# Recurrent rows turned inside the mixer's loop, first gate pieces placed around the last attention units, and a shorter wait ahead of the output projection

## What is computed

```python
y_m = mlstm_chunkwise(q_m, k_m, v_m, log_i, log_f)      # 4 recurrent heads, 256 wide each
y_m = sigmoid(o_m) * y_m
y_a = chunk_causal_mla_attention(q_nope, q_rope, k_nope, k_rope, v_a)   # 8 heads, 128 wide each
g_m, g_a = split(sigmoid(gate_pre), 2)
merged = g_m * (y_m @ w_branch_m) + g_a * (y_a @ w_branch_a)
x = x + gate1 * (merged @ w_out)
```

## Time and profile before

| what | value |
|---|---|
| median of 3 runs (lowest, highest) | 1639.94 us (1638.41, 1641.69) |
| span of the profiled execution | 1638.2 us |
| PE busy | 1520.7 us, 93% of the span |
| DVE, ACT, POOL busy | 47%, 28%, 35% |
| share of PE in the chain that ended last | 84% |
| recurrent loop, first to last unit, with the latent thirds | 871.4 to 938.2 us |
| `yT` strips turned and split | 938.2 to 945.2 us |
| `gm`, `bm` | 945.2 to 1033.2 us |
| attention loop | 1087.5 to 1169.8 us |
| last `yaT` strips | 1170.7 to 1173.4 us |
| `ga`, `ba` | 1173.4 to 1262.2 us |
| `wout` begins | 1266.9 us |

### The profile page before, as it was taken

One profiled execution on the slowest core, in us unless ns is written; L12 is line 12 of the kernel. 1 busy time (PEld: TensorE's weight loads), 2 busy tenths in 40 slices (PEclk: granted clock), 3 DMA queues, 4 the chain that ended last, 5 costly groups with the idle time before them and its releaser, 6 DMA issues.

```text
span 1638.2 us, 21248 instructions
## 1 busy us (share of the span) xinstructions
PE 1520.7 (93%) x8362; PEld 1199.8 (73%) x8362; DVE 769.3 (47%) x1470; ACT 455.3 (28%) x722; POOL 579.8 (35%) x473
## 2 busy tenths in 40 slices
PE   6989998999999999989999999999999989887885
PEld 5978887878888888857888878775688866554442
DVE  2475656378686863238215620445313254423234
ACT  4352334242231313143323232342223121000001
POOL 2571220435454444434533144520154323312222
PEclk9998999999999999989999999999999999989997
DMA  4241110325435442313222122210043689999995
GB/s 166 91 185 49 52 52 1 111 109 212 184 155 206 167 167 103 109 52 109 104 97 71 40 78 103 90 53 23 26 166 143 259 332 353 377 397 373 394 412 200
DMA packets 37347, 260.91 MB, mean 159 GB/s; under 512 B 7280, under 2 KB 7920, under 8 KB 13184
## 3 DMA queue, kind: packets, MB, share of 16 engines
q1 hardware_dynamic: 31488, 251.13, 40.7%
q0 software_dynamic: 5760, 8.41, 1.6%
HBM read 252.69 MB, written 17.30 MB: 165 GB/s over the span
## 4 chain that ended last, share of the span: by engine, by line
PE 84%; DVE 7%; issue 4%; ACT 3%; POOL 1%; DMA 1%; DVEq 0%; SPq 0%; ACTq 0%; POOLq 0%
PE G L2090 13%; PE G L2091 13%; PE G L2092 13%; PE G L2624 4%; PE SA L2624 4%; PE SA L2090 3%; PE SA L2092 3%; PE SA L2091 3%; PE PB L2092 3%; PE PB L2091 3%; PE PB L2090 3%; PE OB L2280 2%; PE G L2132 2%; PE SA L2513 1%; PE PB L2632 1%
## 5 line engine op out<-in xcount | busy, mean ns | idle before, releaser
L753 POOL TENSOR_TENSOR wl<-raw,wh 128x512 fp32r<-128x512 f32 x356 | 479.9, 1379 | 674.5 <-ACT wh L885 669.6
L885 ACT ACTIVATE wh<-raw 128x2048 fp32r<-128x2048 f32 x90 | 172.3, 1915 | 298.7 <-PE SA L2092 153.7
L2090 PE MATMUL G<-Hh,wh 128*128 128x512 f32 x544 | 217.7, 400 | 4.6 <-DVE Yl L1837 1.6
L2091 PE MATMUL G<-Hl,wh 128*128 128x512 f32 x544 | 214.4, 394 | 0.0
L2092 PE MATMUL G<-Hh,wl 128*128 128x512 f32 x544 | 214.3, 394 | 0.0
L1593 DVE SCALAR_TENSOR_TENSOR arena<-arena,st 128x256 f32<-128x256 f32 x144 | 132.9, 923 | 5.1
L2090 PEld LDWEIGHTS G<-Hh,wh 128*128 128x128 f32 x544 | 103.8, 191 | 25.7 <-DVE Yl L1837 1.9
L2092 PEld LDWEIGHTS G<-Hh,wl 128*128 128x128 f32 x544 | 103.5, 190 | 22.6
L2091 PEld LDWEIGHTS G<-Hl,wh 128*128 128x128 f32 x544 | 103.6, 190 | 19.9
L825 POOL DMA_INDIRECT raw<-xn_rows,arena x38 | 36.8, 967 | 129.4 <-PE G L2640 104.9
L2090 PE MATMUL G<-wh,Hh 128*128 128x256 f32 x256 | 76.6, 299 | 0.0
(11 more groups left out here) (528 smaller groups left out, 3111.5 us busy)
## 6 DMA issues: line engine op xcount, KB each, us to landing
raw<-in_pieces_dram SPq DMA_DIRECT2D x91, 1024.0 KB, 4.8
arena<-in_pieces_dram SPq DMA_DIRECT2D x24, 1024.0 KB, 4.8
arena<-in_wexp_dram SPq DMA_DIRECT2D x11, 2048.0 KB
dn_w<-in_wexp_dram SPq DMA_DIRECT2D x18, 1024.0 KB, 42.0
arena<-in_wexp_dram SPq DMA_DIRECT2D x12, 1024.0 KB, 30.3
gu_y<-in_wexp_dram SPq DMA_DIRECT2D x6, 2048.0 KB
gu_z<-in_wexp_dram SPq DMA_DIRECT2D x5, 2048.0 KB
gu_h<-in_wexp_dram SPq DMA_DIRECT2D x4, 2048.0 KB
```

What stands on the lines that cost most here:

```text
L753: ins = pool.tensor_tensor(low_[:, part], whole[:, part], high[:, part], ALU.subtract)
L885: act.activation(split_pair(s)[0], wait_raw(act, sp_list[s]), ACT.Copy).then_inc(S("high_split"), 1)
L2090: pe.matmul(out, ah, bh, start=first, stop=False)
L2091: pe.matmul(out, ah, bl, start=False, stop=False)
```

## The change

- **Recurrent rows.** Strips 0 and 1 (head 0) are turned at the end of step 8, strips 2 and 3 (head 1) at the end of step 12, strips 4 and 5 (head 2) in step 17. Strips 6 and 7 (head 3) are turned between the first and the second `gm` group. The latent thirds 16 and 17 stand inside steps 16 and 17, each ahead of an `mvalues`. ACT and DVE split the strips at their steps 9, 13 and 17. The PE loop has 18 steps. `bm`'s first group waits strip by strip.
- **Latent rows.** The sums of squares stand behind the second `gm` group on ACT and write to another scratch tile; POOL makes the roots behind the split of three more pieces instead of one; DVE scales behind the fourth `bm` group.
- **Attention.** The first `ga` group is cut in two halves: k 0 to 3 ahead of the last `avalues`, k 4 to 7 behind it. The strips of block 3 are turned behind it, then comes the second `ga` group.
- **Output projection.** Pieces 0 and 2 wait for four strips of `merged`, pieces 1 and 3 for all eight.

```diff
     g += [("vm", t, "a") for t in range(8)]
-    g += [("c3", t, "a") for t in range(6)]
-    g += [("yT", f, "v") for f in range(KT)]
+    for i in range(6):
+        g += [("c3", i, "a")]
+        if i in (2, 4, 5):
+            g += [("yT", 2 * (i // 2 - 1) + n + (2 if i == 5 else 0), "v") for n in range(2)]
+    g += [("gm", 0, "a"), ("yT", 6, "v"), ("yT", 7, "v"), ("gm", 1, "a")]
...
-    g += [("yaT", i, "v") for i in range(8)]
+    g += [("yaT", i, "v") for i in range(6)]
+    g += [("ga", 0, "a"), ("yaT", 6, "v"), ("yaT", 7, "v"), ("ga", 1, "a")]
...
+        MIXED_AT = {9: (0, 1), 13: (2, 3), 17: (4, 5)}
...
-            low(sp_list[NC3])
+            for p in sp_list[NC3:NC3 + 3]:
+                low(p)
             pool.wait_ge(S("ss_c"), 1)
...
+            def mixed_high(f):
+                b = wait_group(act, "yT", f)
+                act.activation(Yhv[:, f, :], b[:, :], ACT.Copy, scale=0.5).then_inc(S("yT_high"), 1)
...
                 if t < len(munits):
                     munit(t)
+                if t in MIXED_AT:
+                    for f in MIXED_AT[t]:
+                        mixed_high(f)
...
                     free_group(act.activation(tg[:, f, :], b[:, :], ACT.Tanh, scale=0.5), "gm", i)
+                    if i == 0:
+                        mixed_high(6)
+                        mixed_high(7)
                 high(s)
                 s += 1
+                if j == 0:
+                    latent_squares()
...
             for j in range(4):
                 high(s)
                 s += 1
...
                     free_group(act.activation(tga[:, f, :], b[:, :], ACT.Tanh, scale=0.5), "ga", i)
+                    if i == 0:
+                        attended_high(3)
...
+            def mixed_low(f):
+                b = wait_group(dve, "yT", f)
+                dve.wait_ge(S("yT_high"), f + 1)
+                free_group(dve.scalar_tensor_tensor(Ylv[:, f, :], b[:, :], 0.5, Yhv[:, f, :].bitcast(F32), ALU.mult, ALU.subtract), "yT", f)
...
                 if 0 <= t - 1 < len(munits):
                     mcopied(t - 1)
+                if t in MIXED_AT:
+                    for f in MIXED_AT[t]:
+                        mixed_low(f)
+            mixed_low(6)
+            mixed_low(7)
...
-            for t in range(len(munits) + 3):
+            def mixed_turned(h):
+
+                pe.wait_ge(S("m_out"), 4 * h + 4)
+                for f in range(2 * h, 2 * h + 2):
+                    transposes("yT", f, [To[:, t, f * P:(f + 1) * P] for t in range(NT)])
+
+            for t in range(len(munits) + 2):
                 if t < len(munits):
                     mscores(t)
                 if t < 16:
                     c3_third(t)
+                if t == 17:
+                    c3_third(17)
+                    mixed_turned(2)
                 if 0 <= t - 1 < len(munits):
                     mturned(t - 1)
+                if t == 16:
+                    c3_third(16)
                 if 0 <= t - 2 < len(munits):
                     mvalues(t - 2)
-            for t in (16, 17):
-                c3_third(t)
-            pe.wait_ge(S("m_out"), len(munits))
-            for f in range(KT):
-                transposes("yT", f, [To[:, t, f * P:(f + 1) * P] for t in range(NT)])
-            wait_freed(pe, "yT", KT - 1)
+                if t in (8, 12):
+                    mixed_turned(t // 4 - 2)
+            one_feature("gm", ("gm", 0), 0, 0)
+            mixed_turned(3)
+            one_feature("gm", ("gm", 0), 1, 1)
             for j in range(4):
-                features("gm", ("gm", j), 2 * j)
-                features("bm", ("bm", j), 2 * j, act=(Yhv, Ylv))
+                if j:
+                    features("gm", ("gm", j), 2 * j)
+                features("bm", ("bm", j), 2 * j, act=(Yhv, Ylv), source=None if j else "yT")
...
-            for t in range(len(aunits) + 4):
...
+            for t in range(len(aunits) + 2):
...
+                if t == len(aunits) + 1:
+                    one_feature("ga", ("ga", 0), 0, 0, range(4))
                 if 0 <= t - 2 < len(aunits):
                     avalues(t - 2)
+            one_feature("ga", ("ga", 0), 0, 0, range(4, KT))
+            attended_turned(3)
+            one_feature("ga", ("ga", 0), 1, 1)
             wait_freed(pe, "yaT", 7)
...
-            pe.wait_ge(S("merged_low"), KT)
             for j in range(4):
+                pe.wait_ge(S("merged_low"), KT if j % 2 else KT // 2)
                 wide_rows("wout", ("wout", j), 4 * (j // 2), j % 2)
```

More of the change, by code:

```diff
@@ L188, in plan_groups @@
     g += [("va", i, "a") for i in (6, 7)]
-    g += [("yaT", i, "v") for i in range(8)]
+    g += [("yaT", i, "v") for i in range(6)]
+    g += [("ga", 0, "a"), ("yaT", 6, "v"), ("yaT", 7, "v"), ("ga", 1, "a")]
     for j in range(4):
-        g += [("ga", 2 * j + f, "a") for f in range(2)]
+        if j:
+            g += [("ga", 2 * j + f, "a") for f in range(2)]
         g += [("ba", 2 * j + f, "v") for f in range(2)]
@@ L813, in _ @@
             pool.tensor_tensor(rsc, msc, mhalf.to_broadcast([P, 8]), ALU.pow).then_inc(S("rstd_c"), 1)
-            for p in sp_list[NC3 + 1:]:
+            for p in sp_list[NC3 + 3:]:
                 low(p)
@@ L1160, in aunit, with attended_high @@
                                accum_out=rsum2[:, (q % 2) * 8 + h:(q % 2) * 8 + h + 1]).then_inc(S("probs_ready"), 1)
+            def attended_high(q):
+                for i in range(2):
+                    b = wait_group(act, "yaT", 2 * q + i)
+                    act.activation(Yhv[:, 4 * i:4 * i + 4, q * P:(q + 1) * P], b[:, :].rearrange("p (f n) -> p f n", f=4), ACT.Copy).then_inc(S("yaT_high"), 1)
             for t in range(len(aunits) + 4):
@@ L1167, in _ @@
                     aunit(t)
-                if t >= 11 and (t - 11) % 8 == 0:
-                    q = (t - 11) // 8
-                    for i in range(2):
-                        b = wait_group(act, "yaT", 2 * q + i)
-                        act.activation(Yhv[:, 4 * i:4 * i + 4, q * P:(q + 1) * P], b[:, :].rearrange("p (f n) -> p f n", f=4), ACT.Copy).then_inc(S("yaT_high"), 1)
+                if t >= 11 and (t - 11) % 8 == 0 and t < len(aunits):
+                    attended_high((t - 11) // 8)
             for j in range(4):
@@ L1760, in _ @@
                 free_group(dve.scalar_tensor_tensor(merged[:, i, :], tg[:, i % 2, :], 1.0, b[:, :], ALU.add, ALU.mult), "bm", i)
+                if i == 3:
+                    dve.wait_ge(S("rstd_c"), 1)
+                    for t in range(NT):
+                        dve.tensor_scalar(c3[:, t, 0:CQ], c3[:, t, 0:CQ], rsc[:, t:t + 1], None, ALU.mult)
+                        ins = dve.tensor_scalar(c3[:, t, CQ:CQ + CKV], c3[:, t, CQ:CQ + CKV], rsc[:, 4 + t:5 + t], None, ALU.mult)
+                    ins.then_inc(S("kr_normed"), 1)
             for f in range(5):
@@ L2363, in _, with one_feature, features @@
             pe.wait_ge(S("sml_done"), 2)
-            def features(what, p, i0, ng=2, act=None, kts=range(KT), ncols=PC):
+            def one_feature(what, p, i, f, steps=range(KT)):
+                a, b = (w.rearrange("p (k n) -> p k n", n=PC) for w in weights(p))
+                bank = group(what, i) if steps[0] == 0 else BANKS[WHERE[GIDX[what, i]]]
+                for k in steps:
+                    ins = split3(bank[:, :], (a[:, k, f * P:(f + 1) * P], b[:, k, f * P:(f + 1) * P]), (Hhv[:, k, :], Hlv[:, k, :]),
+                                 k == 0, k == KT - 1)
+                if steps[-1] == KT - 1:
+                    filled(ins)
+            def features(what, p, i0, ng=2, act=None, kts=range(KT), ncols=PC, source=None):
                 h, l = act or (Hhv, Hlv)
@@ L2372, in features @@
                     for kk, k in enumerate(kts):
+                        if source is not None and f == 0:
+                            wait_freed(pe, source, k)
                         ins = split3(bank[:, :], (a[:, kk, f * P:(f + 1) * P], b[:, kk, f * P:(f + 1) * P]), (h[:, k, :], l[:, k, :]),
@@ L2533, in avalues, with attended_turned @@
                 ins.then_inc(S("values_summed"), 1)
-            for t in range(len(aunits) + 4):
+            def attended_turned(q):
+                pe.wait_ge(S("a_out"), 8 * q + 8)
+                for i in range(2):
+                    transposes("yaT", 2 * q + i, [ya[:, (4 * i + f) * P:(4 * i + f + 1) * P] for f in range(4)])
+            for t in range(len(aunits) + 2):
                 if t < len(aunits):
@@ L2540, in _ @@
                 if t >= 11 and (t - 11) % 8 == 0:
-                    q = (t - 11) // 8
-                    pe.wait_ge(S("a_out"), 8 * q + 8)
-                    for i in range(2):
-                        transposes("yaT", 2 * q + i, [ya[:, (4 * i + f) * P:(4 * i + f + 1) * P] for f in range(4)])
+                    attended_turned((t - 11) // 8)
+                if t == len(aunits) + 1:
+                    one_feature("ga", ("ga", 0), 0, 0, range(4))
```

(6 more changed lines are left out.)

26 lines of the change are left out of this document (8 added, 18 removed).

## The result

The changed kernel takes **1629.36 us** (median of 4 runs, 1627.98 to 1631.18) against 1639.18 us of the kernel before in the same session (4 runs). The ratio on record is 0.9936, 95% interval 0.9921 to 0.9952: a gain of 10.5 us (7.9 to 13.0); the two medians shown here lie 9.8 us apart. The profiled execution took 1629.6 us, its span is 1627.6 us against 1638.2.

A forecast was written before the change was run, and what follows sets the result against it. PE bounds the kernel, busy 1520.7 of 1638.2 us. Gains of 3.5 (recurrent loop), 5.0 (attention) and 0 (output projection) sum to 8.5 us, taking the median of 1639.94 to 1631.4 us, range 1628.8 to 1635.8.

The forecast's parts named there:

- wait of step 14: Recurrent loop: ACT's copy of strip 3 waits for latent group 4's number, delaying PE's values(12); costs 1.9 us, bounds 0 to 3.8.
- part 1: Recurrent loop: closing PE's holes gains 5.4 us, less 1.9 for a new wait, so 3.5 us.
- part 2: Attention's end, values(30) to `ba`: gate products cover the waits, 18.98 us becomes 13.94, a gain of 5.0 us.
- of it the clock: Attention's end: the share of the 5.0 us gain beyond waits of about 3.4; without it the gain is 3.3.
- part 3: Output projection: waiting for four strips instead of eight saves 0, since the wait for eight had passed already.
- rival A: Recurrent loop: no wait in step 14 because the strips are ready; gain 10.4 us, 1629.5 us, chance 0.08.
- Rival B: Recurrent loop: DVE becomes the bound, splits delay `mout` in steps 9, 13, 17; 4 us loss, 1635.4 us, chance 0.12.
- rival C: Behind step 14 and at `gm` 1: the clock falls at the turns, costing 3.4 us; 1634.8 us, chance 0.08.
- rival D: Last stage: expert weights' loads bound it and give the gain back; no change, 1639.9 us, chance 0.05.
- E: Step 14's wait to the end of `gm` 1: clock stays at its lower level, 23 us, 1654 us, chance 0.03.
- Queues behind: Loads and expert weights: they are released by progress and move with PE, so the last stage starts earlier as a whole.

The follow-up runs named there:

- e10: The kernel before with five idle products (128 x 256) in the holes around the last attention strips; 1637.76 us, ratio 0.9976.
- e4: The changed kernel with the output projection waiting for all eight strips again; 1630.21 us, ratio 0.9944 against the kernel before.
- e1: The changed kernel with strips 2 and 3 numbered ahead of latent group 4 and turned in step 11; 1629.39 us, ratio 0.9946 against the kernel before.
- e6: The changed kernel with 64 extra turns in step 12 ahead of strip 2; one execution of 1636.21 us.
- e2: The changed kernel with the old attention end, so only the recurrent part and output wait; 1637.77 us, ratio 0.9988 against the kernel before.
- e7: e1 with ACT copying the first row block of the small products ahead of its split of strip 6; 1629.67 us, ratio 0.9942.
- e8: e7 with the output projection waiting for all eight strips; 1630.69 us, ratio 0.9933 against the kernel before.
- e11: The same kernel as e2 measured again, the changed one with the old attention end; 1635.5 us, ratio 0.9971 against the kernel before.
- e3: The changed kernel with the old recurrent loop, keeping the new attention end and output wait; 1634.66 us, ratio 0.997 against the kernel before.
- e5: The kernel before with twelve idle products (128 x 256) in the holes around the last attention strips; 1640.71 us, ratio 1.0007.

## Why the prediction was right in its mechanism, and short in its size

| step of the prediction | forecast | measured |
|---|---|---|
| `mturned(15)` to `bm` | 19.98 | 19.88 |
| wait of step 14, turns to values(12) against before | 1.9 | 1.9 (2.12 against 0.22) |
| part 1, gain of the stretch | 3.5 | 3.47 |
| values(30) to `ba` | 13.94 | 13.86 |
| part 2, gain | 5.0 | 5.12 |
| of it the clock | 1.7 | 1.6 (e10) |
| part 3 | 0 | 0 (e4) |
| sum of the changed stretches | 8.5 | 8.6 |
| everything else | 0 | 2.05 in the profiles, of it 0.7 to 0.9 in places where it recurs; 1.4 by all runs (0.2 to 2.5) |

- **The sum's terms held**, each to 0.1 us or so. What made that possible was laying PE's new order out product by product at the paces of the earlier trace rows and asking at each reader which instruction releases it. One reading was off without harm: what the prediction calls 6 and 8 value products are the two records each of 3 and 4 products (`mvalues` has q+1 of them); the sum goes by records and stands.
- **The time alone would have misled.** 1629.36 us is what rival A forecast (1629.5). The trace has the wait of step 14 that A denies, so the nearness is chance: the wait's 1.9 us were spent and about as much came from elsewhere.
- **Rival A** (no wait) fell in the trace, and e1 shows that the wait hangs on the group's number. **Rival B** (DVE bounds the loop) fell with e1, **rival C** (turns lower the clock) with e6, **rival D** (the last stage gives it back) with the table of stretches: the expert stage began 8.2 us earlier and ended 10.6 earlier. **E** had nothing behind it; no rearranged stretch shows a clock under 1.00.
- **The step that failed** is "Queues behind": "the last stage starts earlier as a whole", and with it a term of 0 in the sum for every stage whose order is unchanged, with "about 0.7 us on either side" for scatter. In the first pair of profiles those stages gave 2.05 us (0.65 ahead of the loop, 0.20 from `bm` to values(30), 1.2 from `wout` to the end), by all runs 1.4. Not only do they scatter, by 2.0 us in the expert stage and 6.3 at the start of the loop in profiles of one program; a part recurs. Where the hole at the attention's end is closed, the way to `slots` some 150 us later is also 0.5 to 0.7 us shorter in ten of eleven profiles, with less of it at the lower clock. So the mechanism of the change was right, and the term for the rest of the program was mis-sized.
- **What stays open** is how much of the term lasts beyond those 0.7 to 0.9 us. The six profiles that show the lower clock somewhere between the loop and `wout` (before, e1, e2, e7, e8, e11) have expert stages of 293.7 to 296.0 us, mean 294.5; the eight that do not have 291.6 to 294.9, mean 292.7. That looks like 1.8 us more, but the wait ahead of the stage takes it back: from `slots` to the end the means are 303.7 and 303.4. The partial kernels show no more either, 3.4 us (e2, e11) and 4.9 (e3) where their stretches have 3.5 and 5.1; only e10 does, 3.9 us where its stretch has 1.6 (2.5 by the medians). The mean granted clock of a whole run points to the clock: 0.976 in the 15 runs of the changed kernel, 0.973 in the 60 runs of before beside the experiments (e4's five have 0.974). No run changed the clock in those stages alone, so why it falls less there is not shown.

## What to carry to other kernels

A counter that readers compare with a group's number orders work that has nothing to do with each other: when a step is moved, move its number too, or the reader waits for a stranger. A hole in the bottleneck engine is filled best with products that are due anyway, cut in pieces ahead of each wait; idle ones keep the clock as well, but must fit the hole. Where the work is laid out at measured paces the changed stretch can be forecast to a tenth of a microsecond; the margin of the total belongs to the stages that nobody touched. And before a stage is called shorter, its border is moved to an instruction that waits for nothing new: here a gain of 2.5 us shrank to 0.5.

## What was not expected of the hardware

- Float32 products show two records each and cost twice the one record's time: 0.43 us for 128 x 256 in `SA` (e5, e10), and the same in `OB`, where the four products of values(15) are the x8 of the earlier trace rows.
- The clock does not follow from a hole's length alone. At the latent strips PE stands 0.65 and 1.64 us in e1 and goes on at 1.2 GHz, for the eight products at 0.43 us each; with holes as long at the same place it stays at 1.00 in the changed kernel. The busy time by stretch there, of the changed kernel:

```profile
1024.00:1040.00 16.00, 13.72 (x69) 10.94 (x68) 9.37 (x14) 6.20 (x8) 6.67 (x6) 1.00 0.21 75
```

and of e1:

```profile
1024.00:1037.00 13.00, 10.72 (x49) 8.22 (x48) 9.01 (x13) 5.66 (x8) 5.16 (x4) 0.87 0.23 85
```

PE is idle 2.28 us in both. With 1.95 us gained 80 us earlier, 1.65 us are lost here, in all three kernels of that kind and in none of the other eleven. Why is not shown.
